# A two-block model on one core: what is transferred first, who issues the side inputs, and the order of the first products

## The reference

```python
h = rmsnorm(x, attn_norm_g[l])
proj = h @ w_in[l]                      # 256x1024 @ 1024x3072
dq, dk, dv, rq, rk, rv, rg = jnp.split(proj, SPLIT_POINTS, axis=-1)
dq = rotate_prefix(dq..., pos, rope_inv); dk = rotate_prefix(dk..., pos, rope_inv)
...                                     # differential attention on dq, dk, dv
log_gamma = -jnp.exp(ret_log_decay[l])
r_fwd = retention_direction(rq, rk, rv, log_gamma[0], False)
r_bwd = retention_direction(reversed rq, rk, rv, log_gamma[1], True)
...
mix = jnp.concatenate([a, r], axis=-1)
x = x + mix @ w_out[l]
x = x + peer_ffn(rmsnorm(x, ffn_norm_g[l]), ...)   # experts
```

## Time and profile before

| | |
|---|---|
| three runs | 1542.40, 1542.82, 1545.98 us (median 1542.82) |
| profiled execution | 1544.33 us, of which the span from first to last instruction is 1542.2 us |
| granted TensorE clock, mean | 0.993 |
| PE busy | 1496.8 us, 97% of the span |
| POOL, DVE, ACT busy | 62%, 55%, 49% of the span |
| moved | 254 MB, mean 165 GB/s |

### The profile page before, as it was taken

The page is one execution under the profiler, slowest core; times in us unless marked ns, Lnnn a source line. Parts: engine busy times, 40 slices in busy tenths (PEclk is TensorE's granted clock), DMA queues, the critical chain, the costliest instruction groups (busy, mean ns, idle before and its releaser), DMA issues.

```text
span 1542.2 us, 26608 instructions
## 1 busy us (share of the span) xinstructions
PE 1496.8 (97%) x9614; PEld 1348.1 (87%) x9614; DVE 842.7 (55%) x2082; ACT 760.4 (49%) x1270; POOL 958.4 (62%) x409
## 2 busy tenths in 40 slices
PE   7999999999999999999999999998999999999997
PEld 6678998999999888889999999987899689899996
DVE  4555189989998655532222222244577634366565
ACT  6456545454444554444444444456656355544444
POOL 6547787874554000048888888877744256588885
PEclk9999999999999999999999999999999899999999
DMA  7434567663333666656566666666533244366653
GB/s 245 133 110 137 177 180 231 191 179 105 116 110 124 192 193 193 196 176 185 188 189 183 186 190 186 183 200 193 178 110 97 96 124 150 111 185 183 188 183 118
DMA packets 69489, 254.17 MB, mean 165 GB/s; under 512 B 7776, under 2 KB 8032, under 8 KB 68768
## 3 DMA queue, kind: packets, MB, share of 16 engines
q1 hardware_dynamic: 67248, 244.35, 51.8%
q10 hardware_dynamic: 1728, 6.68, 1.2%
q0 software_dynamic: 432, 2.07, 0.4%
HBM read 249.91 MB, written 3.15 MB: 164 GB/s over the span
## 4 chain that ended last, share of the span: by engine, by line
PE 60%; issue 21%; POOL 16%; DVE 2%; ACT 1%; DMA 1%; POOLq 0%; ACTq 0%; DVEq 0%
PE bank L484 19%; PE bank L485 19%; PE bank L486 19%; POOL w_lo L449 15%; PE bank L875 4%; DMA ring<-weights_in 1%; POOL w_lo L443 0%; POOLq L459 0%; ACT w_hi L1358 0%; ACT h_hi L1427 0%; DVE xres L2064 0%; POOLq L448 0%; DVE work L2417 0%; DVE w_lo L2448 0%; DVE act_lo L2453 0%
## 5 line engine op out<-in xcount | busy, mean ns | idle before, releaser
L449 POOL TENSOR_TENSOR w_lo<-ring,w_hi 128x1024 fp32r<-128x1024 f32 x392 | 940.5, 2402 | 558.0 <-ACT w_hi L1358 550.9
L1358 ACT CAST w_hi<-ring 128x1024 fp32r<-128x1024 f32 x452 | 473.9, 1050 | 626.5 <-PE bank L486 586.5
L484 PE MATMUL bank<-h_hi,w_hi 128*128 128x256 f32 x1696 | 487.7, 288 | 4.3 <-POOL w_lo L449 3.3
L486 PE MATMUL bank<-h_hi,w_lo 128*128 128x256 f32 x1696 | 479.7, 283 | 0.0
L485 PE MATMUL bank<-h_lo,w_hi 128*128 128x256 f32 x1696 | 479.6, 283 | 0.0
L484 PEld LDWEIGHTS bank<-h_hi,w_hi 128*128 128x128 f32 x1696 | 324.6, 191 | 9.0 <-POOL w_lo L449 4.1
L485 PEld LDWEIGHTS bank<-h_lo,w_hi 128*128 128x128 f32 x1696 | 324.8, 192 | 3.5
L486 PEld LDWEIGHTS bank<-h_hi,w_lo 128*128 128x128 f32 x1696 | 324.4, 191 | 0.0
L484 PE MATMUL bank<-w_hi,act_hi 128*128 128x512 f32 x600 | 234.9, 392 | 4.4 <-DVE act_lo L2453 1.5
L485 PE MATMUL bank<-w_lo,act_hi 128*128 128x512 f32 x600 | 234.5, 391 | 0.0
L486 PE MATMUL bank<-w_hi,act_lo 128*128 128x512 f32 x600 | 233.5, 389 | 0.0
(11 more groups left out here) (406 smaller groups left out, 1853.5 us busy)
## 6 DMA issues: line engine op xcount, KB each, us to landing
ring<-weights_in SPq DMA_DIRECT2D x463, 512.0 KB, 3.6
mem_kv<-arena ACTq DMA_DIRECT2D x2, 1024.0 KB, 7.2
arena<-mem_kv ACTq DMA_DIRECT2D x2, 1024.0 KB, 6.2
xres<-x_in SPq DMA_DIRECT2D x2, 512.0 KB, 6.7
arena<-mem_in POOLq DMA_DIRECT2D x1, 1024.0 KB, 9.4
arena<-rows_in ACTq DMA_DIRECT2D x2, 512.0 KB, 5.1
arena<-consts_in POOLq DMA_DIRECT2D x1, 512.0 KB, 11.3
arena<-consts_in ACTq DMA_DIRECT2D x2, 256.0 KB, 5.5
```

What stands on the lines that cost most here:

```text
L449: nc.gpsimd.tensor_tensor(w_lo[:, k, :], ring[:, k, :], w_hi[:, k, :].bitcast(F32), ALU.subtract)\
L484: pe.matmul(out_, a[0], b[0], start=start, stop=False, **kw)
L486: return pe.matmul(out_, a[1], b[0], start=False, stop=stop, **kw)
L1358: nc.scalar.copy(w_hi[:, k, :], ring[:, k, :]).then_inc(s["hi_made"], 1)
```

## The change

The first half of x is transferred first, then the second, then slots 0, 1, 2. SP issues rows behind slot 2, the distance tables behind slot 3, mem and the positions behind slot 4. POOL issues only `mix_gain`, behind slot 13. ACT casts slots 0, 1, 2, 3 behind blocks 0, 3, 5, 7 of h_hi; slot 3 is thus cast ahead of the squares of x, slot 4 behind them, and slots 5 and 6 behind the two squares of mem. PE takes slots 0 to 3 in a new function that starts when w_hi is there: eight matmuls with w_hi (h_hi and h_lo), then the wait for w_lo, then four with w_lo.

```diff
-            sp.dma_start(ring[:, 0, :], weights[SOURCE[0]]).then_inc(loaded[0], 16)
             sp.dma_start(xres[:, 0, :], x_in[:, 0, :]).then_inc(s["x_loaded"], 16)
             sp.dma_start(xres[:, 1, :], x_in[:, 1, :]).then_inc(s["x_rest_loaded"], 16)
-            for n in range(1, N_SLOTS):
+            for n in range(N_SLOTS):
                 if n >= NR:
                     sp.wait_ge(s["split"], n + 1 - NR)
                 sp.dma_start(ring[:, n % NR, :], weights[SOURCE[n]]).then_inc(loaded[n % NR], 16)
+                if n == NR - 1:
+                    sp.dma_start(rows[:, :], rows_in[:, 0:NROWS]).then_inc(s["rows_loaded"], 16)
+                elif n == NR:
+                    sp.dma_start(area("later_earlier"), consts[:, NCONST:NCONST + 1024]).then_inc(s["later_loaded"], 16)
+                elif n == NR + 1:
+                    sp.dma_start(mem[:, :, :], mem_in).then_inc(s["mem_loaded"], 16)
+                    sp.dma_start(pos_i[:, :], pos_in).then_inc(s["pos_loaded"], 16)
...
-            lo_part(0, 0)
-            pool.dma_start(rows[:, :], rows_in[:, 0:NROWS]).then_inc(s["rows_loaded"], 16)
-            pool.dma_start(mem[:, :, :], mem_in).then_inc(s["mem_loaded"], 16)
-            pool.dma_start(area("later_earlier"), consts[:, NCONST:NCONST + 1024]).then_inc(s["later_loaded"], 16)
-            pool.dma_start(pos_i[:, :], pos_in).then_inc(s["pos_loaded"], 16)
+            lo_parts(0, STEP["w_in"] + 14)
             pool.dma_start(mix_gain[:, :], ...).then_inc(s["gain_row_loaded"], 16)
-            lo_parts(1, DVE_FIRST)
+            lo_parts(STEP["w_in"] + 14, DVE_FIRST)
...
-            for i in range(8):
-                in_unit(i)
+            def first_panel(n):
+                pe.wait_ge(s["hi_made"], n + 1)
+                part = lambda a, k, t: h_t[a][:, k, t * P:(t + 1) * P]
+                weight = lambda a, half: w_parts[a][:, n % NS, half * 512:half * 512 + 512]
+                for half in range(2):
+                    k = 2 * n + half
+                    low("attn_norm", k)
+                    for t in range(TT):
+                        pe.matmul(bank[:, t, :], part(0, k, t), weight(0, half), start=(k == 0), stop=False)
+                        pe.matmul(bank[:, t, :], part(1, k, t), weight(0, half), start=False, stop=False)
+                wait_slot(pe, n)
+                for half in range(2):
+                    k = 2 * n + half
+                    for t in range(TT):
+                        mm = pe.matmul(bank[:, t, :], part(0, k, t), weight(1, half), start=False, stop=(k == KD - 1))
+                mm.then_inc(s["spent"], 1)
+            for n in range(4):
+                first_panel(n)
...
-            hi_parts(1)
             act.wait_ge(s["cols_loaded"], 16)
             for b in range(KD):
...
                 nc.scalar.mul(h_t[0][:, b, :], bank[:, to, c:c + T], col("attn_g", b)).then_inc(s["split_act"], 1)
-                if b == 1:
-                    hi_parts(2)
-            hi_parts(NS)
+                if b in CAST_AFTER:                      # (0, 3, 5, 7)
+                    hi_parts(CAST_AFTER.index(b) + 1)
             norm_sums(NORMS["attn"], xres)
-            hi_parts(NS + 1)
+            hi_parts(NS + 2)
...
-                hi_parts(NS + 2 + t)
+                hi_parts(NS + 3 + t)
```

More of the change, by code:

```diff
@@ L186 @@
 RAW_AT = [(4, 0), (5, 0), (6, 0), (7, 0), (0, 0), (1, 0), (2, 0), (3, 0)]
+CAST_AFTER = (0, 3, 5, 7)
 FIRST_AT = [(4, 0), (5, 0), (6, 0), (7, 0), (2, 0), (2, T), (3, 0), (3, T)]
```

## The result

| | before | after |
|---|---|---|
| median of 20 runs | 1546.04 us | 1552.10 us |
| lowest and highest | 1540.43, 1547.58 | 1544.04, 1558.82 |
| ratio after / before | | 1.0036, 95% interval 1.0025 to 1.0048 |
| profiled execution, span | 1542.2 us | 1542.4 us |

What follows compares the result with a forecast made beforehand. PE was taken to bound the kernel, with the chain ACT, DVE, ACT, POOL setting its time at slot 7. +1.9 there and +1.4 for the clock made +3.3: 1542.8 + 3.3 = 1546.1, stated as 1546 us, range 1541 to 1548.5.

Steps and rivals of the forecast that it cites:

- +1.9 for slot 7: Through slot 7: 1.0 gained at the start, 0.85 from waits, 3.75 lost as lead and delay; net +1.9 us.
- +1.4 for the clock: Behind the standstill at slot 7: PE's clock falls to half rate, costing 1.4 us.
- The first h_hi came 2.26 after PE's start, that is 0.3 after its last transpose; now it comes at 8.0.: Start of the kernel: x arrives earlier, first h_hi at 8.0, PE's first weight matmul at 9.95 instead of 10.97.
- The chain behind it: ACT, DVE, ACT, POOL up to slot 7: squares of x 2.35 us later, slot 7 split at 36.25.
- PE behind slot 3: PE from slot 4 (22.8) to slot 7: a lead of 2.0 us ends in a standstill of 4.35 us.
- so they cost nothing, but with only 0.2 to 0.9 us to spare: Side inputs on SP's queue: mem and slots 4 to 6 land before they are needed, at no cost.
- Rival (c): Transfers late: mem or slot 5 lands 1.5 us after need, standstill 5.9 us, time 1547.6 to 1549; chance 0.15.
- DVE's waits for POOL's subtraction: In ACT's chain: DVE's mean and lambda product wait for POOL, coming at 26.4 and 28.9; shift 1.95 us either way.
- rival (a): Same standstill at slot 7, but the clock stays: 1544.7; chance 0.15.
- (b): At slot 7 PE's lead lives, POOL having split the slot by 31.9: -1.9 us, 1540.9; chance 0.13.
- (d): Early gain and later wait cancel, the chain being about 2 us shorter: 1542.8; chance 0.07.

Runs made afterwards that it cites:

- early table: Changed kernel plus one 128x1 copy on ACT once the identity is there, so its function table loads early; ratio to the kernel before 1.0026.
- x first alone: Kernel before with only the two halves of x transferred ahead of slot 0; ratio to the kernel before 1.0004.
- 36 transposes: Changed kernel with 36 more transposes of the identity, read by nothing, ahead of PE's slot 7; ratio to the kernel before 1.0030.
- 18 transposes: Changed kernel with 18 more transposes of the identity, read by nothing, ahead of PE's slot 7; ratio to the kernel before 1.0023.
- all three together: Changed kernel with table loaded early, squares of x ahead of slot 3's cast, mem and positions issued behind rows; ratio to the kernel before 1.0000.
- Squares first, alone: Changed kernel with the squares of x ahead of slot 3's cast again, every later cast one place later; ratio to the kernel before 1.0023.
- the casts of slots 7 and 8 first: Changed kernel with decay_exp(0) on ACT behind the casts of slots 7 and 8 instead of ahead; ratio to the kernel before 1.0032.
- the three repairs and the casts first: Changed kernel with early table, squares first, mem issued early, and decay_exp(0) behind the casts of slots 7 and 8; ratio to the kernel before 1.0000.

## Why the prediction was wrong

The direction and the place (a standstill of PE at slot 7, set by ACT's chain, with the clock low behind it) were right; the size was not, nor was the head of the chain. I forecast +3.3 us and 1546.0, measured were +5.6 and 1552.1, outside my range of 1541 to 1548.5. Of the 6.1 us between forecast and measurement 3.2 lie in the median of three runs that I started from, which was bad luck, 2.3 in the change's cost, the rest in rounding and in a ratio that is not that of the two medians. From the median of 20 the same sum gives 1549.3 and a range up to 1551.7, still short of 1552.1. The ratio's interval (+0.25 to +0.48%) also lies mostly above 0.3%, and to a kernel slower by more than that I had given a chance of 0.20. Of the two terms, +1.9 for slot 7 was 3.35 in the first pair of profiles and 4.5 in the second, and +1.4 for the clock was 1.6 and 2.2.

- **"The first h_hi came 2.26 after PE's start, that is 0.3 after its last transpose; now it comes at 8.0."** This step failed, and it is the largest part of the missed size: the sum has nothing for ACT's function table. The first h_hi came at 9.61. The identity landed at 6.05 and not at 5.35, and the first half of x at 5.8 and not at 5.2. 0.3 of the 1.6 us are due to that; the rest of that delay is hidden, as PE waits for the second half of x anyway. The other 1.28 us are the table load. In the kernel before it ran under ACT's wait for slot 0, in front of the cast of slot 0. The change moves that cast behind the first h_hi, so the first instruction that needs a table is now that h_hi, and the load stands behind its waits. I had listed the cast as moved and not the load in front of it. The early table showed it alone: h_hi at 8.36.
- **The chain behind it** then held in its order and its lengths, but late: the cast of slot 3 at 17.13 (forecast 15.9), the squares at 18.09 (16.85), the square of mem at 22.95 (21.75), decay_arg(0) at 33.64 (32.2), slot 7 at 37.71 (36.25), each 1.2 to 1.5 late. The table load is 1.04 of that at the cast of slot 3 and at the squares, as the early table shows (16.09 and 17.05). Behind the squares it no longer counts alone, as mem's landing held ACT until 22.69 even without it. What is left, 0.2 to 0.4 us, has no run of its own.
- **"PE behind slot 3"**: I had PE 1.7 ahead at slot 4 (22.8) and 2.0 ahead when it met the wait of slot 7. It was 0.4 behind at slot 4 (24.94) and 0.6 ahead at the end of slot 6, because its first weight matmul came at 11.07 (forecast 9.95) and the eight of slot 0 with w_hi ran at half rate. The standstill of 4.35 us was one of 4.12 all the same, since slot 7 was late as well. That the two errors nearly cancel in the standstill is luck. In the loss only the lateness of slot 7 counts.
- **"so they cost nothing, but with only 0.2 to 0.9 us to spare"**, of the side inputs. In the first profile they held up ACT by 0.17 us (slot 5), in the second ACT waited 0.65 us for mem, and with the table or the squares repaired it waited 0.71 and 2.82. Rival (c), transfers 1.5 us late, was present as a second bound next to the first; that its price (+4.8 to +6.2) takes in the measured 5.6 is luck, as mem was never that late. The page DMA: Bandwidth & Descriptors of the Trainium skill, Issuing engines are not separate DMA queues, says that the transfers of all issuers run on the same 16 engines, and that a further issuer saves only the issuing. The runs are in keeping with it: issued by POOL (x first alone, at 13.0) mem took 6.8 us, issued by SP (kernel after, at 16.2) 6.7. It landed at 22.9 instead of 18.7 because it was issued 6.9 us later.
- **DVE's waits for POOL's subtraction**, which I had assumed, are now seen in thirteen more profiles: the mean took 1.30 to 1.36 us and the product 2.1 to 2.2, each ending with a subtraction. These two always stood alike to POOL, so their length alone proves little. The mean of x's norm, an instruction of the same form, does more: it took 0.24 to 0.26 us in ten profiles, 0.51 to 0.53 in three and 0.95 in one, and ended within 0.1 us of the end of a subtraction each time (in the last one by a third of a merged row).
- **The clock**: forecast 1.4 us, measured 1.6 in the first profile and 2.2 in the second. The kernel with 36 transposes shows that the clock stays when the standstill is filled. It does not show that such a long one is needed: 2.15 us were enough with 18 transposes, and once 0.86. The Trainium skill, TensorE: Matmul & The Clock Gate, HAM oscillation, told the sign; the size is the rows'. What I gave for rival (a), that PE's first work ran at 1.00, was a misreading (see the last section).
- Rivals (b) and (d) fall: no lead lived. Rival (a) falls with the clock.

## What to carry to other kernels

When an instruction moves on an engine that needs function tables, ask which instruction is now the first to need one, and what the load hides behind there: here a load of 1.28 us went from under a transfer onto the path, and 1.04 of it reached the chain. Ask of a move how far it pushes the slowest chain that later work of the same engine stands behind, not only what it gives the busiest engine: PE was given 1.45 us of head start and lost 5, because ACT casts slot 7 behind a chain of norms. And where two bounds end at the same time, repair both before a part is judged: at slot 7 each alone gave 0.25 to 0.35 us against the first profile of the kernel after, all three together 4.3. Squares first, alone, had a first score 1.8 us earlier only because its low clock fell into another place.

## What the runs showed of the hardware that I had not expected

- PE runs at half rate at the start, and the profile's stretches print a clock of 1.00 there. The spacing tells it: the 16 first transposes took 3.4 to 3.7 us in every kernel, 0.21 to 0.23 each, and the 36 transposes of the same size in the middle of a kernel took 4.09 us, 0.11 each. In the first profile of the kernel after, the first weight matmuls still came 0.43 apart, after a wait of 1.35 us in front of them (printed clock 1.00); in the second, behind a wait of 1.55 us, and with the casts of slots 7 and 8 first, behind one of 1.35, they came at full rate.
- How long the clock stays low behind a standstill differs between executions of one kernel (in the two profiles of the kernel after 3.4 and 6.8 us at slot 7; in the two of the kernel before 13.6 us in one piece at 1200 us, and 3.4 and 6.8 us in two). Such stretches are worth up to half their length, 1.7 to 6.8 us each, and make up most of the spread of 7 to 15 us between the runs of one kernel: the fastest and the slowest of the kernel after (1544.04 and 1558.82 us) have mean clocks of 0.995 and 0.987, a difference of about 12.5 us of the 14.8. For a change at the start, a mark soon behind it tells more than a pair of spans.
- How long PE has to stand still for it differs too. The clock fell behind 2.15 us in the kernel with 18 transposes and behind 0.86 us with the three repairs and the casts first; behind 0.86 us it stayed with the three repairs alone, and behind 1.22 to 1.49 us, three times, with only the casts first.
- The identity, on ACT's queue, landed 0.7 us later (5.3 instead of 4.6 us after its issue) when SP's first two transfers were x instead of a weight slot and half of x, though the bytes on SP's queue are the same (1 MB). Why was not tried.
